# Hybrid decoder, one core: the sample's projections moved into the output of each layer's last tile

## What is computed

```python
def hybrid_layer(x, c, pos0, k_buf, v_buf, shift_prev, wkv0, conv_buf, h0, lp):
    mod = jax.nn.silu(c) @ lp["w_mod"] + lp["b_mod"]
    shift_m, scale_m, gate_m = jnp.split(mod, 3, axis=-1)
    h = rmsnorm(x, lp["norm_pre"]) * (1.0 + scale_m[:, None]) + shift_m[:, None]
    proj = h @ lp["w_in"]                       # 2880 columns
    qa, ka, va, ga, pb, gb, xc, gc = jnp.split(proj, IN_OFFSETS, axis=-1)
    ...                                         # A: attention over a window of 128
    yb, shift_new, wkv_new = rwkv7_time_mix(pb, gb, shift_prev, wkv0, lp)
    yc, conv_new, h_new = rglru_mix(xc, gc, conv_buf, h0, pos0, lp)
    y = jnp.concatenate([ya, yb, yc], axis=-1) @ lp["w_out"]
    x = x + gate_m[:, None] * rmsnorm(y, lp["norm_post"])
```

## Time and profile before

| | us |
|---|---|
| median of 3 runs | 2826.74 (2822.93 to 2827.25) |
| profiled execution, its own time | 2828.5 |
| span of the profile | 2826.6 |
| TensorE busy | 2742.0 (97%) |
| VectorE busy | 1704.8 (60%) |
| ScalarE busy | 1338.2 (47%) |
| GpSimd busy | 254.9 (9%) |
| mean granted TensorE clock | 0.98 of full |

### The profile page before, as it was taken

The page is one execution under the profiler, slowest core; times in us unless marked ns, Lnnn a source line. Parts: engine busy times, 40 slices in busy tenths (PEclk is TensorE's granted clock), DMA queues, the critical chain, the costliest instruction groups (busy, mean ns, idle before and its releaser), DMA issues.

```text
span 2826.6 us, 64205 instructions
## 1 busy us (share of the span) xinstructions
PE 2742.0 (97%) x25404; PEld 2017.2 (71%) x25404; DVE 1704.8 (60%) x4627; ACT 1338.2 (47%) x3136; POOL 254.9 (9%) x357
## 2 busy tenths in 40 slices
PE   6999999999999999999889999999999999999987
PEld 5777777777777777776577777777777777777754
DVE  2666666666666666666246666666666666666664
ACT  2545445455544454554144555444445544445442
POOL 0000111011001110110000100011011000110010
PEclk8999999999999999999889999999999999999998
DMA  9200000000000000001770000000000000000002
GB/s 361 90 17 25 23 25 9 24 25 24 17 24 24 24 10 24 24 17 33 213 239 17 24 25 17 25 24 25 9 24 25 24 17 24 24 24 9 17 16 45
DMA packets 62139, 119.23 MB, mean 42 GB/s; under 512 B 15232, under 2 KB 35200, under 8 KB 61568
## 3 DMA queue, kind: packets, MB, share of 16 engines
q1 hardware_dynamic: 55792, 113.64, 12.2%
q10 hardware_dynamic: 6032, 1.12, 0.2%
HBM read 96.34 MB, written 18.41 MB: 41 GB/s over the span
## 4 chain that ended last, share of the span: by engine, by line
PE 93%; DVE 3%; DMA 2%; issue 1%; ACT 1%; POOL 0%; DVEq 0%; POOLq 0%; SPq 0%; ACTq 0%
PE G L503 17%; PE G L629 17%; PE M L851 16%; PE G L498 8%; PE M L498 5%; PE M L678 5%; PE M L494 4%; PE M L691 3%; PE G L745 2%; PE G L509 1%; PE M L657 1%; PE M L727 1%; PE G L494 1%; DMA RB<-in_w_mod 1%; DVE Q L1621 1%
## 5 line engine op out<-in xcount | busy, mean ns | idle before, releaser
L503 PE MATMUL G<-hT,w_in 128*128 128x128 f32 x4224 | 507.1, 278 | 3.3 <-issue 3.3
L503 PEld LDWEIGHTS G<-hT,w_in 128*128 128x128 f32 x4224 | 494.9, 195 | 21.5 <-issue 16.4
L629 PE MATMUL G<-hT,w_in 128*128 128x256 f32 (+1 forms) x2048 | 497.1, 385 | 0.0
L851 PE MATMUL M<-w_out,yT 128*128 128x512 f32 x1024 | 455.5, 598 | 2.8 <-DVE yT L1761 2.8
L629 PEld LDWEIGHTS G<-hT,w_in 128*128 128x128 f32 x2048 | 360.4, 189 | 64.7 <-issue 12.3
L851 PEld LDWEIGHTS M<-w_out,yT 128*128 128x128 f32 x1024 | 193.9, 192 | 222.6 <-issue 221.0
L498 PE MATMUL G<-w_in,hT 128*128 128x512 f32 x512 | 244.2, 609 | 0.0
L1621 DVE TENSOR_TENSOR Q<-Q,M 64x256 f32<-64x256 f32 x320 | 133.8, 418 | 130.4 <-PE M L691 127.2
L678 PEld LDWEIGHTS M<-W 64*64 64x64 f32 x4608 | 147.6, 135 | 24.3 <-issue 24.3
L1381 POOL TENSOR_TENSOR RA<-RA,small 128x1024 f32<-128x1024 f32 x32 | 60.6, 1895 | 1134.2 <-DVE small L1673 1134.2
L678 PE MATMUL M<-W 64*64 64x64 f32 x4608 | 162.7, 219 | 0.0
(11 more groups left out here) (445 smaller groups left out, 4546.1 us busy)
## 6 DMA issues: line engine op xcount, KB each, us to landing
w_in<-in_w_in SPq DMA_DIRECT2D x8, 2048.0 KB, 15.5
w_out<-in_w_out SPq DMA_DIRECT2D x2, 4096.0 KB, 20.4
G<-in_x_prompt SPq DMA_DIRECT2D x16, 512.0 KB, 3.5
x_mid<-RA SPq DMA_DIRECT2D x16, 512.0 KB, 2.9
G<-x_mid SPq DMA_DIRECT2D x16, 512.0 KB, 3.3
out_y_prompt<-RA SPq DMA_DIRECT2D x16, 512.0 KB, 2.8
xa<-in_x_prompt SPq DMA_DIRECT2D x15, 512.0 KB, 3.7
xa<-x_mid SPq DMA_DIRECT2D x15, 512.0 KB, 3.8
```

What stands on the lines that cost most here:

```text
L503: last = mm(out[0:width, :], Win[:, k, col:col + width], H[:, k, :], start=k == 0, stop=k == KC - 1)
L629: last = mm(out, Win[:, k, col:col + P], moving, start=k == 0, stop=k == KC - 1)
L851: last = mm(o[:, :], yT[:, k, :], Wout[:, k, 512 * h:512 * h + 512], start=k == 0, stop=k == KC - 1)
```

## The change

The six row groups and their foldings leave the sample step and go into the last tile of each layer. Rows 0 and 1 stand before the transposes of y; foldings 0 and 1 with rows 2 and 3 stand between the two projection halves; foldings 2 and 3 with rows 4 and 5 follow half 1, and foldings 4 and 5 come after that (in layer 0 after chunks 12 to 15). Rows go to banks M0 and M1, foldings to G0. The modulation's chunks are dealt to other banks (`MB`) and grouped by fours around these steps.

For this the sample's norm moves forward into the tile body: VectorE clears `dhp` and squares behind `bonus_out`, TensorE sums before multiply(2), VectorE makes "ms" behind the rotary step, ScalarE takes the root in front of power(4), and VectorE makes the scaled input (`sample_scaled`) behind the LRU's scan. VectorE copies all six row groups in `copy_rows()`, in the place of `sample_input()`, ahead of its wait for `o_root`. Buffers that the moved steps would overwrite are replaced by parts of `stBC` and `stA`. SP's program stays as it is. The diff, cut to its core:

```diff
-        dsq = stA[:, 0:64].rearrange("p (c b) -> p c b", b=B)
-        dhp = Q[:, :, :].rearrange("p u c -> p (u c)").rearrange("p (k b) -> p k b", b=CG)
+        dsq = stBC[:, 0, 0, 0:64].rearrange("p (c b) -> p c b", b=B)
+        dhp = stBC[:, 0, 2:4, :].rearrange("p a t -> p (a t)").rearrange("p (k b) -> p k b", b=CG)
-        dr1, dr2, dm = stA[:, 240:248], stA[:, 248:256], stA[:, 256:264]
+        dr1, dr2, dm = stBC[:, 0, 0, 64:72], stBC[:, 0, 0, 72:80], stA[:, 256:264]
-        srow = [xs[:, 0:4, :].rearrange("p k t -> p (k t)"), qk[:, 0:512]]
+        srow = [xs[:, 0:4, :].rearrange("p k t -> p (k t)"), stA[:, :]]
+        orow = [srow[0], qk[:, 0:512]]
-        MB = (M0, M1, G0, M2, M0, M1)
+        MB = (M4, M2, G1, M3, M2, G1)
...
+                def sample_rows(g):
+                    col, width, _ = DGROUPS[g]
+                    column_groups((M0, M1)[g % 2][:, 0:width], dhp, lambda k: Win[:, k, col:col + width]).then_inc(L["row_mm"], 1)
+
+                def sample_channels(g):
+                    first, _, chunks = DGROUPS[g]
+                    return to_channels(srow[g % 2], MODG + l * (ROWS - MODG) + g, G0, B,
+                                       [(DCHUNKS[j][0] - first, DCHUNKS[j][1], B * j) for j in chunks])
...
                     multiply(1)
                     squares(2)
                     filler(1)
+                    if not ahead:
+                        pe.wait_ge(smp["dve"], AT("sq", l))
+                        for k in range(KC):
+                            last = mm(M4[:, 0:B], con("reset")[:, 1:2].to_broadcast([P, P]), dsq[:, k, :], start=k == 0,
+                                      stop=k == KC - 1)
+                        last.then_inc(smp["pe"], 1)
                     multiply(2)
                     squares(3)
                     filler(2)
                     pe.wait_ge(s["rope_ready"], DONE(n))
                     pe.wait_ge(s["bt_out"], DONE(n))
+                    if not ahead:
+                        pe.wait_ge(smp["dve"], AT("ms", l))
...
                     if fused:
                         pe.wait_ge(L["padded"], 2)
-                        mod_chunks(0, 1, 2, 3, 4, 5)
+                        mod_chunks(0, 1, 2, 3)
+                    if not ahead:
+                        pe.wait_ge(smp["dve"], AT("h", l))
+                        sample_rows(0)
+                        sample_rows(1)
 
                     pe.wait_ge(s["yn_ready"], DONE(n))
...
                     if fused:
-                        mod_chunks(6, 7)
                         mod_fold(0)
+                        mod_chunks(4, 5, 6, 7)
...
                     if ahead:
                         front(n + 1)
                     else:
-                        pe.wait_ge(smp["dve"], AT("sq", l))
-                        for k in range(KC):
-                            last = mm(M3[:, 0:B], con("reset")[:, 1:2].to_broadcast([P, P]), dsq[:, k, :], start=k == 0,
-                                      stop=k == KC - 1)
-                        last.then_inc(smp["pe"], 1)
+                        pe.wait_ge(s["gbc_out"], DONE(n))
+                        sample_channels(0)
+                        sample_rows(2)
+                        sample_channels(1)
+                        sample_rows(3)
                     if fused:
-                        pe.wait_ge(s["gbc_out"], DONE(n))
                         mod_chunks(8, 9, 10, 11)
                         mod_fold(1)
-                        mod_chunks(12, 13)
+                        pe.wait_ge(L["mod_act"], MFOLD[0])
                     project(1, M4).then_inc(s["o1_mm"], 1)
+                    if not ahead:
+                        sample_channels(2)
+                        sample_rows(4)
+                        sample_channels(3)
+                        sample_rows(5)
                     if fused:
-                        mod_chunks(14, 15)
+                        mod_chunks(12, 13, 14, 15)
                         mod_fold(2)
-                        pe.wait_ge(L["mod_act"], MFOLD[0])
+                    if not ahead:
+                        sample_channels(4)
+                        sample_channels(5).then_inc(smp["pe"], 1)
+                    if fused:
+                        pe.wait_ge(L["mod_act"], MFOLD[1])
                         mod_chunks(16, 17, 18, 19)
                         mod_fold(3)
-                        pe.wait_ge(L["mod_act"], MFOLD[1])
+                        pe.wait_ge(L["mod_act"], MFOLD[2])
                         mod_chunks(20, 21, 22, 23)
...
-                pe.wait_ge(smp["dve"], AT("h", l))
-
-                def proj_channels(g):
...
-                for g, (col, width, _) in enumerate(DGROUPS):
-                    if mixed and g == 1:
-                        pe.wait_ge(L["mod_act"], MFOLD[5])
-                    column_groups((G1, G0)[g % 2][:, 0:width], dhp, lambda k: Win[:, k, col:col + width])\
-                        .then_inc(L["row_mm"], 1)
-                    if g > 0:
-                        proj_channels(g - 1)
-                proj_channels(len(DGROUPS) - 1).then_inc(smp["pe"], 1)
...
                     A(lth, lth, ACT.Sqrt).then_inc(s["lru_root"], 1)
+                    if not ahead:
+                        act.wait_ge(smp["dve"], AT("ms", l))
+                        A(dr2[:, :], dr1[:, :], ACT.Sqrt).then_inc(smp["act"], 1)
                     power(4)
...
-                    else:
-                        act.wait_ge(smp["dve"], AT("ms", l))
-                        A(dr2[:, :], dr1[:, :], ACT.Sqrt).then_inc(smp["act"], 1)
...
-                def sample_input():
-
-                    dl(ms(dhp, 0.0))
-                    signal(tt(dsq[:, :, :], xsT[:, :, :], xsT[:, :, :], ALU.mult), "sq")
-                    dve.wait_ge(smp["pe"], AT("ssq_mm", l))
-                    signal(ts(dr1[:, :], M3[:, 0:B], 1.0 / D, EPS, ALU.mult, ALU.add), "ms")
+                def sample_scaled():
+
                     dve.wait_ge(smp["act"], AT("root", l))
                     dl(rcp(dr2[:, :], dr2[:, :]))
                     dl(tt(dh[:, :, :], xsT[:, :, :], over(dr2[:, :], 1, KC), ALU.mult))
                     dl(tt(dh[:, :, :], dh[:, :, :], gs[:, :, 1:1 + B], ALU.mult))
                     signal(tt(dh[:, :, :], dh[:, :, :], mod[:, 0:8, 1:1 + B], ALU.add), "h")
+
+                def copy_rows():
+                    for g, (_, width, _) in enumerate(DGROUPS):
+                        dve.wait_ge(L["row_mm"], l * (ROWS - MODG) + (g + 1))
+                        cp(srow[g % 2][:, 0:width], (M0, M1)[g % 2][:, 0:width]).then_inc(L["row_out"], 1)
...
                     tt(bonv[:, :], G1[:, 0:256], xsv, ALU.mult).then_inc(s["bonus_out"], 1)
+                    if not ahead:
+                        dl(ms(dhp, 0.0))
+                        signal(tt(dsq[:, :, :], xsT[:, :, :], xsT[:, :, :], ALU.mult), "sq")
...
+                    if not ahead:
+                        dve.wait_ge(smp["pe"], AT("ssq_mm", l))
+                        signal(ts(dr1[:, :], M4[:, 0:B], 1.0 / D, EPS, ALU.mult, ALU.add), "ms")
...
                     cp(hcar[:, :].unsqueeze(2), lh[:, :, P - 1:P])
+                    if not ahead:
+                        sample_scaled()
                     if mixed and not ahead:
                         pad(cnext)
...
                     else:
-                        sample_input()
+                        copy_rows()
 
                     dve.wait_ge(s["o_root"], DONE(n))
...
-                for g, (_, width, _) in enumerate(DGROUPS):
-                    dve.wait_ge(L["row_mm"], l * (ROWS - MODG) + (g + 1))
-                    cp(srow[g % 2][:, 0:width], (G1, G0)[g % 2][:, 0:width]).then_inc(L["row_out"], 1)
-
                 dve.wait_ge(smp["in_small"], (l + 1) * 64)
                 dve.wait_ge(smp["pe"], AT("proj_mm", l))
                 dl(ms(pj[:, 6, :], 0.0))
-                cp(pj[0:64, 6, :], M1[0:64, 6 * B:7 * B])
+                cp(pj[0:64, 6, :], G0[0:64, 6 * B:7 * B])
```

More of the change, by code:

```diff
@@ L994, in _ @@
                 for h in range(2):
-                    last = to_channels(srow[h], MODG + l * (ROWS - MODG) + len(DGROUPS) + h, M3, B, [(P * j, P, B * (4 * h + j)) for j in range(4)])
+                    last = to_channels(orow[h], MODG + l * (ROWS - MODG) + len(DGROUPS) + h, M3, B, [(P * j, P, B * (4 * h + j)) for j in range(4)])
                 last.then_inc(smp["pe"], 1)
@@ L1249, in tile @@
                     act.wait_ge(s["o0_mm"], DONE(n))
-                    A(RB[:, 0:512] if ahead else stB, M5[:, :], ACT.Square, accum_out=small[:, 3:4])
+                    A(RB[:, 0:512] if ahead else qk[:, 0:512], M5[:, :], ACT.Square, accum_out=small[:, 3:4])
                     if ahead:
                         decays(n + 1)
-                    else:
-                        act.wait_ge(smp["dve"], AT("ms", l))
-                        A(dr2[:, :], dr1[:, :], ACT.Sqrt).then_inc(smp["act"], 1)
                     if fused:
@@ L1259, in tile @@
```

(2 more changed lines are left out.)

8 lines of the change are left out of this document (3 added, 5 removed).

## The result

The changed kernel takes 2840.78 us (median of 4 runs, 2840.09 to 2843.33) where the kernel before takes 2825.94 (2822.93 to 2827.25): ratio 1.0056, 95% interval 1.0044 to 1.0068, so 15 us slower. One slow execution of a later kernel, the one without early loads, took 5040.45 us, and its ratio leaves that one out. The profiled executions have spans of 2839.2 and 2826.6, 12.6 us apart, and those 12.6 us divide as follows. The last tile of layer 0 begins 0.8 us sooner, that of layer 1 2.06 us later, so layer 0 costs 2.9 us (forecast 10).

The account below looks back on a forecast made before the run. TensorE looked like the bound, but a DMA branch, `ob`'s store then small loads and state, was nearly as long. Layer 1 +9.2 and layer 0 +10 gave +19 us: median 2845.8, 8-in-10 range 2833 to 2853.

Parts of the forecast that it names:

- The tile body: Last tile, both layers: multiply(4) 1.7 us later, everything from the probabilities on 2.8 us late (bounds 1 and 3.2).
- The sum: Whole kernel: 9.2 us from layer 1 plus 10 from layer 0, +19 us, profiled execution 2847.6, median 2845.8.
- Layer 1: Layer 1's end: `ob` 10.2 us later, the small loads behind its store move along, `pj` +9.2 us (bounds +5 and +12).
- the bulk: Three big loads behind layer 1's small loads, 1.5 MB: there at 2800.2, in time for use 8 us behind `pj`.
- The 15.5: Layer 1: time from `ob` done to small loads landed, 15.5 us (bounds 13.5 and 16.6).
- Layer 0: Layer 0: small loads issued 15 us later, `pj` 2 us sooner, state product late; +10 us in all (bounds +2 and +13).
- the 5 us for half clock: Layer 0, TensorE from chunk 3 to chunk 12: 5 us added for half clock behind waits (bounds 2 and 7).
- The 1.5 us for the next layer's gains: Behind layer 0's state load: the gains that TensorE wants for layer 1 come 1.5 us late.
- Cheaper: Rival, chance 0.22: same branches, but clock up in half 0, shift 1 us, last w_mod loads sooner; +9.7, 2836.4.
- The train shrinks: Rival, chance 0.09: small loads land soon after issue, the rows are hidden; 2825.2, or 2815 with both layers short.
- worse: Rival, chance 0.14: ScalarE's small-weight loads fall into layer 0's train, half clock through the sample chain; 4 us more, 2850.
- `ob` isn't held up: Rival, chance 0.05: `ob` isn't delayed and the tile's waits absorb the rest; 2827.

Follow-up runs that it names:

- the one without early loads: Changed kernel with `ob` ahead of row copies 4 and 5, shift-state store packed, layer 0's state load ahead of x, layer 1's loads unmoved: 2822.88 us, ratio 0.9988.
- the two profiles with the rows behind the tile and the stores as before: Two profiled executions of the changed kernel with its six row groups and foldings put back behind the last tile's work: 2833.59 us, ratio 1.0031.
- the packed store: Changed kernel with the shift state stored from a packed copy, 128 rows of 7 elements, instead of 896 single elements: 2828.62 us, ratio 1.0010.
- with early loads: Changed kernel with `ob` first, packed shift-state store, layer 0's state load ahead of x, and most of layer 1's sample loads issued before `ob`'s store: 2815.79 us, ratio 0.9965.

## Why the prediction was right, and where it was not

**The tile body.** As worked out: multiply(4) waits for ScalarE's power (0.62 us where it had none), the block is 1.5 us late (1.7 forecast), and the values product 2.6 us (2.8).

**The sum.** The profiles are 12.6 us apart, 6.6 less than the forecast of 19.2 before rounding: layer 0 gave 7.1 less, layer 1 0.4 more, the chain behind `pj` 0.95 that the sum didn't have, and 0.8 came off ahead of the last tile of layer 0. The medians, 15 us apart, flatter the forecast by 2.

**Layer 1.** The wait of 4.86 us is down to 1.49, half 0 took 9.62 us (9.0), `ob` was stored 8.6 us behind half 1 (9.0) and 10.3 us later than before (10.2), the small loads landed 15.8 us behind `ob` (15.5), `pj` began 9.6 us late (9.2), the bulk was in time. Each term held within about 0.6 us. The 15.5 was read off a window of 3 us (13.5 to 16.6), so that it was so close has some luck; the two profiles with the rows behind the tile and the stores as before have 15.0 and 14.7. What the prediction left open, why so long, is settled by the packed store.

**Layer 0.** This is the term that failed: 2.9 us and not 10. Chunk 12 ended at 1384.4 and not 1392.3. Its path behind chunk 3 was 35.2 us (35.9 forecast), but the 5 us for half clock were 0, and chunk 3 ended at 1349.2 instead of 1351.4 (its load, issued 1.7 us later than before, landed only 0.65 us later). The prediction took over the clock of before, where TensorE waited 2.90 us and two shorter times and the chunks behind took 1.08 us each. In the changed kernel the same stretch has waits of 1.83 and 0.82 us, with the two row groups and the y transposes between them, and the chunks behind take 0.64: the change itself removed what made the clock fall. By the profiles compared above, both its parts count, the rows that fill the wait and the new order of the chunks, and the second more for half 0. The step should have asked which of the waits the inserted and the moved work fills, as it did in layer 1. The rest held: the stream to chunk 23 took 13.9 us (13 forecast), the small loads went 7.7 us later, `pj` came sooner and the state ended the wait, 22.8 us behind the first small load (23). The 1.5 us for the next layer's gains didn't appear: 1461.39 against 1459.67 is the layer's own delay.

**The rivals.** "Cheaper" (2836.4) was right on layer 0's clock and wrong on layer 1. "The train shrinks" (2825 or 2815, faster) was the right mechanism for another kernel: its conditions, small loads within 6.5 us of `ob` and the state of layer 0 within 14 us, were not met by the change. With the packed store the small loads of layer 1 start `pj` 8.7 us behind `ob` (15.9 in the changed kernel), and with the state moved it is there 16.8 us behind layer 0's first small load. Both still miss the conditions, and the packed store alone gives 2828.62, no gain on the kernel before; with `ob` first and the state moved the kernel turns faster, 2822.88, and with early loads 2815.79. Of "worse" (2850) one mechanism showed, in small and in layer 1: the half clock behind TensorE's idle time is in the 0.95 us of the chain behind `pj`. "`ob` isn't held up" (2827) fell: it came 10.3 us later.

## What to carry to other kernels

Before moving work off the engine that seems to bound a tail, find the second branch and its length: here TensorE's 21 us had a neighbour nearly as long, and hiding them bought nothing while the delay of `ob` moved that neighbour. Read in the DMA view the time from issue to landing of each small load; where 8 KB take 11.6 us while 33 GB/s flow, look for a store of single elements on another queue: here it was one, and packing it was worth 13 us, more than the reorderings that came behind it (6 and 6.5). When work is put into a wait, work out the clock behind it anew.

## What the runs showed of the hardware

A store of 896 single elements (3.5 KB) on ScalarE's queue held up transfers on SP's queue that touch neither its source nor its target: 11.6, 4.2 and 1.7 us for the same 8 KB with the store as it was, packed, and absent; 13.3 and 5.2 us for a key piece of 128 KB with the store as it was and packed. The store itself takes 9.2 to 9.3 us from issue to landing as it was, 2.4 packed. TensorE's granted clock in layer 0 stayed up through waits of 1.83 and 0.82 us, and in another run through one of 3.01; it fell behind waits of 2.41, 0.80 and 1.02 (mean 0.72 over the 6 us from 1355) and was up again for the projection half right behind; with the program of before it was at half for over 10 us, in one run behind waits of 1.91 and 1.78 us only. The length of one wait doesn't tell; what TensorE does between the waits has to be looked at too.
